# A hybrid decoder step on one core: the stretch from the third window attention to the memory attention laid out anew

## The reference

```python
for g, (w, d) in enumerate(B_GROUPS):          # ((128, 1), (512, 4), (2048, 16))
    if wins is None:
        o, lse = _dilated_prompt(qd[:, :, g], k_all[:, :, g], v_all[:, :, g], d, w // d)
    else:
        o, lse = _dilated_decode(qd[:, :, g], wins[g][0], wins[g][1],
                                 k_all[:, :, g], v_all[:, :, g], d, w // d)
    outs.append(o)
    lses.append(lse)
wts = jax.nn.softmax(jnp.stack(lses, axis=0), axis=0)
ydil = jnp.einsum('gbth,gbthd->bthd', wts, jnp.stack(outs, axis=0).astype(jnp.float32))
y_mix = ydil.reshape(B, T, B_WIDTH).astype(x.dtype) * jax.nn.silu(zg)
...
ym = _mem_attention(qm.reshape(B, T, M_HEADS, M_HDIM), mk, mv).reshape(B, T, M_WIDTH) * jax.nn.silu(zm)
out = jnp.concatenate([y_mix, ym], axis=-1) @ w_out
x = x + _rmsnorm(out, p['g_post'][l])
```

## Time and profile before

| | us |
|---|---|
| median of 3 runs | 1996.47 (1989.38 to 1996.92) |
| the profiled execution | 1994.59 |
| its span, first to last instruction | 1992.8 |
| PE busy (94%) | 1882.9 |
| DVE busy (40%) | 795.9 |
| ACT busy (25%) | 502.7 |
| POOL busy (22%) | 444.4 |

### The profile page before, as it was taken

How to read it: one execution, slowest core, us unless ns; L and a number is a source line. 1 busy time by engine, 2 the same in 40 slices (tenths; PEclk the granted TensorE clock), 3 DMA queues, 4 the chain that set the end, 5 groups by cost and what they waited for, 6 DMA issues and landing times.

```text
span 1992.8 us, 20946 instructions
## 1 busy us (share of the span) xinstructions
PE 1882.9 (94%) x8106; PEld 1381.9 (69%) x8117; DVE 795.9 (40%) x1463; ACT 502.7 (25%) x1122; POOL 444.4 (22%) x353
## 2 busy tenths in 40 slices
PE   7999999899999999979999999999999978699798
PEld 4566654687666667746658888888888866578373
DVE  0332202454455523552242552354345324855333
ACT  1412222554233323401210013211211222123211
POOL 0000000110222101230004663276237522122100
PEclk9999999999999999989999999999999988899899
DMA  7321210122756433641111111222233235524322
GB/s 260 106 69 59 69 39 13 55 77 39 225 162 193 153 106 89 171 143 64 44 52 43 43 53 50 80 96 75 64 101 111 88 94 157 173 89 141 121 85 86
DMA packets 163165, 196.13 MB, mean 98 GB/s; under 512 B 19355, under 2 KB 122395, under 8 KB 162930
## 3 DMA queue, kind: packets, MB, share of 16 engines
q1 hardware_dynamic: 135748, 168.83, 26.9%
q10 hardware_dynamic: 27318, 25.95, 4.3%
HBM read 156.97 MB, written 37.85 MB: 98 GB/s over the span
## 4 chain that ended last, share of the span: by engine, by line
PE 85%; DVE 6%; DMA 3%; ACT 3%; issue 2%; POOL 1%; ACTq 1%; SPq 0%; POOLq 0%; DVEq 0%
PE PS L2718 25%; PE PS L301 20%; PE PS L1908 10%; PE PS L502 4%; PE PS L1941 4%; PE PS L1768 3%; PE PS L381 3%; PE PS L1621 2%; PE PS L512 2%; DMA window_outputs<-WK 2%; PE PS L1656 1%; PE PS L1633 1%; PE PS L783 1%; PE PS L775 1%; PE PS L1653 1%
## 5 line engine op out<-in xcount | busy, mean ns | idle before, releaser
L301 PE MATMUL PS<-HT,RING 128*128 128x344 f32 x1344 | 391.2, 453 | 1.6 <-DVE HT L459 1.2
L301 PEld LDWEIGHTS PS<-HT,RING 128*128 128x128 f32 x1344 | 255.0, 190 | 135.7 <-DVE HT L459 2.0
L2718 PE MATMUL PS<-HT,RING 128*128 128x260 f32 (+1 forms) x1152 | 300.3, 389 | 11.0 <-ACT BIG L2802 11.0
L2718 PEld LDWEIGHTS PS<-HT,RING 128*128 128x128 f32 x1152 | 216.1, 195 | 41.0 <-ACT BIG L2802 12.7
L1908 PE MATMUL PS<-BIG 128*128 128x512 f32 x384 | 173.4, 603 | 0.0
L1674 ACT ACTIVATE WK<-PS,WK 128x256 f32<-128x256 f32 (+1 forms) x160 | 68.9, 436 | 237.4 <-DVE WK L1694 237.4
L1908 PEld LDWEIGHTS PS<-BIG 128*128 128x128 f32 x384 | 72.1, 193 | 81.3 <-issue 81.1
L2321 POOL TENSOR_TENSOR RING<-RING,VEC 128x1024 f32<-128x1024 f32 x48 | 92.3, 1947 | 135.6 <-DMA RING<-in_w_in_b 73.8
L2802 ACT ACTIVATE BIG<-PS 128x256 f32<-128x256 f32 (+1 forms) x96 | 37.0, 385 | 302.9 <-PE PS L2718 302.8
L728 POOL TENSOR_TENSOR WK<-WK,CST 128x512 f32<-128x512 f32 x8 | 10.3, 1287 | 422.0 <-DMA WK<-mlstm_rows 422.0
L1694 DVE TENSOR_REDUCE WK<-PS 128x2 f32<-128x512 f32 (+1 forms) x80 | 48.3, 603 | 135.4 <-PE PS L1621 90.6
(11 more groups left out here) (334 smaller groups left out, 2927.9 us busy)
## 6 DMA issues: line engine op xcount, KB each, us to landing
WK<-in_cache_mem_kv SPq DMA_DIRECT2D x64, 256.0 KB, 4.7
RING<-in_w_kv_b SPq DMA_DIRECT2D x12, 1024.0 KB, 5.4
RING<-in_w_in_b SPq DMA_DIRECT2D x12, 1024.0 KB, 5.2
WK<-in_cache_win SPq DMA_DIRECT2D x48, 256.0 KB, 4.8
RING<-in_w_in_a ACTq DMA_DIRECT2D x21, 512.0 KB, 4.2
RING<-in_w_mkv SPq DMA_DIRECT2D x16, 512.0 KB, 4.9
BIG<-in_x_prompt SPq DMA_DIRECT2D x16, 512.0 KB, 3.2
XTRA<-in_state_C SPq DMA_DIRECT2D x32, 256.0 KB, 3.7
```

Of the source, the lines that this page charges most:

```text
L301: last = nc.tensor.matmul(PS[:, s + b, 0:SEG], w[:, kt * P:(kt + 1) * P], rhs(kt, b * SEG, (b + 1) * SEG), start=(kt == 0), stop=(kt == kt ...
L2718: last = nc.tensor.matmul(PS[:, bank, 0:mid - lo], weight_block(u // 2, s, k), h_block(u % 2, t, k), start=(k == 0 and j not in (2, 3, 6)) ...
```

## The change

Stores of the window outputs go from SP to ACT. Row statistics get a buffer of their own, `ROWSTAT`, with four blocks, and are copied into `OUTR` only with the second half of the output, so the wait for the store moves from the maximum to the copy of the output. The eight keys of the third window are loaded by two transfers of four tiles into `LATE_KEYS`, and their queries get three buffers. Of each "D" value ACT multiplies two tiles in 8 instructions of 128x128 (one per head), and DVE multiplies one. "B" gets four key tiles, two query tiles and two product tiles; two of each and more of these lie where pieces 6 and 7 of `w_out_b` go, so these two are loaded by SP after the last key sum. The slots of nearly everything after 257 are set anew, the first two window attentions get a step every 2 slots, and the value places and the DVE order of layer A's output stage are moved.

```diff
+        def whole_group(name, n):
+            return name == "D" and n >= 2 * NS
+        def query_held(name, n):
+            if name == "D":
+                return max(2 * NS, n - 2) if whole_group(name, n) else n
+            return n - (len(SMP[name]["queries"]) - 1) * per_query(name)
...
+            if n == 2 * NS and name == "D":
+                sp.wait_ge(sig("rotated").sem, 24)
+                for half in range(2):
+                    at = slice(4 * half, 4 * half + 4)
+                    sp.dma_start(LATE_KEYS[:, at, :], wins[2][at, :, 0, :].rearrange("b p n -> p b n"))\
+                        .then_inc(key_loaded(name, n + 4 * half)[0], 16)
...
-            for t in range(nt):
+            for t in range(1 if name == "D" else nt):
...
+                if name == "D" and t == 1:
+                    dve.wait_ge(*scaled_by_act("value", b))
...
+        def sample_values_act(act, name, b):
+            c = SMP[name]
+            v = value_tiles(name, b)
+            act.wait_ge(*value_loaded(name, b))
+            for t in range(1, c["nt"]):
+                for h in range(H):
+                    x = v[t][:, h * P:(h + 1) * P]
+                    at = t * HP + h * NS + b
+                    last = nc.scalar.activation(x, x, ACT.Copy, scale=c["m"]["turned"][:, at:at + 1])
+            last.then_inc(sig("scaled_by_act").up(), 1)
...
-                if g not in MEM and s % 2 == 0 and (g > 0 or i >= 2):
-                    dve.wait_ge(*(out_stored(g, i - 2) if i >= 2 else out_stored(g - 1, 6 + i)))
...
+                    if pair == 0 and (g > 0 or i >= 2):
+                        dve.wait_ge(*(out_stored(g, i - 2) if i >= 2 else out_stored(g - 1, 6 + i)))
+                    if pair == 1:
+                        nc.vector.tensor_copy(OUTR[:, i % 2, 512:520], ROWSTAT[:, i % 4, :])
...
-        VALUE_SLOTS = {"A": {(1, 2): 0, (1, 4): 1, (1, 6): 2, (0, 9): 3, (0, 11): 4, (1, 9): 5, (1, 11): 6, (2, 1): 7},
+        VALUE_SLOTS = {"A": {(1, 2): 0, (1, 3): 1, (1, 5): 2, (1, 6): 3, (0, 8): 4, (0, 9): 5, (0, 11): 6, (1, 8): 7},
...
-            first, second = (5, 8) if x == "A" else (2, 5)
+            first, second = (8, 8) if x == "A" else (2, 5)
...
-            if a < 3:
-                return 84 * (a + 1) + 5 + 5 * s // 3
-            return 313 + 3 * s // 2
+            if a < 2:
+                return 84 * (a + 1) + 5 + 2 * s
+            return 257 + 3 * s // 2 if a == 2 else 315 + 4 * s // 3
...
-            return 84 * (g + 1) + 20 + 7 * j if g < 2 else 266 + 3 * j
+            return 84 * (g + 1) + 20 + 7 * j if g < 2 else 265 + 2 * j
...
-            return [b for b in range(NS) if 292 + 2 * b == x]
+            return [b for b in range(NS) if 286 + 3 * b == x]
...
-            return [c for c in range(8) if 291 + 2 * c == x]
-        SHARES, SCORES_D, PROBS_D, TURN_MKV, QUERY_B, B_KEYS = 287, 288, 291, 311, 312, 313
+            return [c for c in range(8) if 292 + 5 * c // 2 == x]
+        SHARES, SCORES_D, PROBS_D, TURN_MKV, QUERY_B, B_KEYS = 284, 283, 285, 314, 315, 316
...
-        def store_outputs(sp, g, i):
-            sp.wait_ge(*count("out_read", unit(g, 2 * i + 2)))
-            sp.dma_start(output_rows(g, i), OUTR[:, i % 2, :]).then_inc(sig(f"outputs{i % 2}_saved").sem, 16)
+        def store_outputs(act, g, i):
+            act.wait_ge(*count("out_read", unit(g, 2 * i + 2)))
+            act.dma_start(output_rows(g, i), OUTR[:, i % 2, :]).then_inc(sig(f"outputs{i % 2}_saved").sem, 16)
...
+            sp.wait_ge(sig("key_sums").sem, SMP["B"]["base"] + 2 * NS)
+            for n in range(6, KT):
+                load_piece(sp, n)
...
-            for c in merged_at(x - 4):
+            for c in merged_at(x - 3):
                 merged_turn_pe(pe, c)
...
+                for w, s in steps_at(x - 1):
+                    if w < 3 and s >= 3 and s % 2 == 1:
+                        store_outputs(act, w, (s - 3) // 2)
...
-                for c in merged_at(x):
+                for c in merged_at(x - 1):
                     merge_dve(dve, c)
-                for b in values_at(x):
+                for b in values_at(x - 1):
                     sample_values_dve(dve, "D", b)
...
-                if B_KEYS + 4 <= x < SLOTS and x % 3 == 1:
+                if B_KEYS + 4 <= x < SLOTS and x % 2 == 1:
```

More of the change, by code:

```diff
@@ L1215, in build @@
         tile_loaded = [sig(f"tile{n}_loaded") for n in range(4)]
-        query_loaded = [sig(f"query{n}_loaded") for n in range(2)]
+        query_loaded = [sig(f"query{n}_loaded") for n in range(3)]
         def samples(name, nt, base, key, value, query, tiles, queries, prods, misc, free, new=None, bank=None,
@@ L1264, in count_loads @@
                 for k in range(c["nt"] * NS):
-                    buf = k % len(c["tiles"])
-                    n[buf] += 16
+                    buf = key_buffer(name, k)
+                    if not whole_group(name, k) or k % 4 == 0:
+                        n[buf] += 16
                     LOADS[name, "key", k] = n[buf]
@@ L2433, in stat_of @@
                 return NMAX[:, 2 * s:2 * s + 2], TOTAL[:, 2 * s:2 * s + 2]
[L2434 removed]
+            return tuple(ROWSTAT[:, i % 4, at + 2 * pair:at + 2 * pair + 2] for at in (0, 4))
         def out_stored(g, i):
@@ L2519, in layer_b_sp @@
                     store_rows(sp, g, i)
-                for w, s in steps_at(x - 1):
-                    if w < 3 and s >= 3 and s % 2 == 1:
-                        store_outputs(sp, w, (s - 3) // 2)
-                for n in keys_at(x + 6):
-                    if n % NS == 0:
-                        sp.wait_ge(sig("query_rows_saved_d").sem, 16 * (n // NS + 1))
+                for n in keys_at(x + 5):
                     sample_load(sp, "D", n)
+                if x == SHARES - 1:
+                    sp.wait_ge(*count("out_ready", unit(2, 16)))
+                    for b in range(2):
+                        value_load(sp, "D", b)
                 if x == SHARES:
@@ L2534, in layer_b_sp @@
                         load_merge(sp, c)
-                    for b in range(2):
-                        value_load(sp, "D", b)
                     sp.wait_ge(sig("rotated").sem, 24)
@@ L2563, in layer_b_sp, with load_piece @@
             out_sp(sp, "B")
+        def load_piece(engine, n):
+            engine.dma_start(OUT["B"].piece(n), a["w_out_b"][0][n * P:(n + 1) * P, :])\
+                .then_inc(sig("out_weights_loaded").sem, 16)
         def rotated_before(u):
@@ L2803, in product_copy_act, with scaled_by_act @@
                                  ACT.Copy).then_inc(sig("projections_copied").up(), 1)
+        def scaled_by_act(kind, n):
+            order = [(what, k) for x in range(SLOTS) for what, at in (("merge", merged_at), ("value", values_at)) for k in at(x)]
+            return sig("scaled_by_act").sem, order.index((kind, n)) + 1
         def merged_act(act, c):
@@ L2853, in layer_b_act @@
                     act.wait_ge(sig("yd_ready").sem, 1)
-                if n >= 0 and n % 2 == 0 and n // 2 < KT:
-                    n //= 2
-                    act.dma_start(OUT["B"].piece(n), a["w_out_b"][0][n * P:(n + 1) * P, :])\
-                        .then_inc(sig("out_weights_loaded").sem, 16)
+                if n >= 0 and n % 2 == 0 and n // 2 < 6:
+                    load_piece(act, n // 2)
             complete(act, NUNIT - 1)
```

59 lines of the change are left out of this document (38 added, 21 removed).

## The result

The changed kernel takes 1923.95 us (median of 4 runs, 1922.78 to 1924.54) against 1995.39 for the kernel before beside it: ratio 0.9647, 95% interval 0.9626 to 0.9668. The profiled execution takes 1923.77 us with a span of 1921.7; before, it was 1994.59 and 1992.8. The forecast was 1920.

What follows compares the result with a forecast made beforehand. PE, 94% busy, was taken to lose time to waits and the half clock behind them. Gains 14.3 + 7.5 + 20.5 + 23.5 + 0 + 8.8 = 74.6 us from 1994.6 give 1920 us, range 1900 to 1944.

Steps and rivals of the forecast that it cites:

- Layer A's output stage: PE's 10.83 us wait for value 5 and the half clock behind it go; gain 14.3 us, bounds 0 and 14.3.
- First two attentions: First two window attentions: exp gets 1.74 us more, waits for late stores go; gain 7.5 us, bounds 3 to 8.7.
- Third attention: Third window attention: ACT's stores, keys without waits and later buffer reuse end the store waits; gain 20.5 us, bounds 8 to 22.
- Rival 3: Stores land late rather than issue late, third attention keeps its 20.5: 1940; or layer A's values come late: 1934; chance 0.09.
- Rival 4: ACT, in order at stores, value and merge loads, holds everything and its late copies stop PE: 2040 us; chance 0.03.
- From the softmax of "D" to the memory attention: DVE sheds value multiplies to ACT and only its bursts hold PE; gain 23.5 us, 16 of 39.5 left, bounds 5 to 36.
- Merge loads land in 4.3 us: Softmax of "D" to memory attention: merge loads have 2 slots, costing 0 to 1 us each on ACT, unseen by PE.
- The 8 us for POOL's pass over pair 22: Behind slot 293, POOL's pass over weight pair 22 slows a merge from 2.31 to 6.27 us; 8 us for wait and half clock.
- Rival 1: DVE stays the bound behind slot 283, 26 to 32 us lost there instead of 16: about 1933 us; chance 0.20.
- rival 2: Clean stretch behind slot 283: loss shrinks from 16 to 5 us, third attention's from 3.4 to 1.5: 1907; chance 0.10.
- Memory attention: Memory attention, 70.4 us: steps closer but same work, no gain taken; bounds -4 and 2 us.
- Layer B's output stage: Start of layer B's stage: "B" key sum wait and half clock go (13.1), waiting for `w_out_b` pieces costs 4.3; gain 8.8, bounds 3 to 13.

Runs made afterwards that it cites:

- the run of its two lines alone: The kernel before with only layer A's value places and DVE's order in its output stage as changed; 1980.88 us, ratio 0.9925.
- the run of the split wait: The changed kernel with the wait for pieces 6 and 7 of `w_out_b` moved to where they are used; 1915.23 us, ratio 0.9611.

## Why the prediction was right, and where its steps were not

The time came out as forecast, and six of the seven stretches of the table to within 1 us. Agreement that close is in part luck: the same stretches of the kernel before differ by up to 4 us between two executions, and the forecast was summed from the one execution with which the table compares. Of the mechanisms, that of layer A's stage was right as it stood, those of the third attention and of layer B's stage in part.

*Layer A's output stage.* Right, 14.2 for 14.3 (14.4 from the stage's first matmul on), and shown by the run of its two lines alone.

*First two attentions.* Right, 2.8 and 4.8. Which of the moved steps brings it was not taken apart further; the stores alone bring 1.0 and 3.1 of it (100.5 and 92.2 us between the same slots).

*Third attention.* The size was right, 21.0 for 20.5, but I named three things that take the turn of the earlier trace rows apart as if all three were needed. The stores on ACT alone give all of it, and the rest of the change gives it without them. The statistics apart and the later copy give nothing measurable beside the stores on ACT. Rival 3, that a store is late because it lands late and so the move does nothing, saw something true that I had passed over: the three stores that held DVE for 18.4 of its 25.4 us did land late, in 5.0 to 6.6 us. It falls all the same, because this too came from the place behind a load, and went with the move. I had read 2.6 us from copy to issue in the earlier trace rows and stopped there, where the landing had the larger part. As to the sentence of the Trainium skill that I weighed there (DMA: Bandwidth & Descriptors, Issuing engines are not separate DMA queues), that a second issuing engine only saves the time of starting transfers: the move gave 22 us here, not the 8 us of issue, as the stores no longer stood at another transfer's wait, nor landed behind it.

*Rival 4, ACT as the queue that holds everything.* ACT carries 24 stores and 64 scalings more and takes 39.06 us of 88.20; PE never waits for an ACT copy of a product there, and with the stores back on SP the time is the same.

*From the softmax of "D" to the memory attention.* I left 16 of 39.5 us. Between the slots 20.1 are gained, so 19.4 are left; but the stretch also holds less work, 118 woven matmul records for 141, and at the 0.11 us of one in the forecast that is 2.5 us which only moved to the stretches on either side (10 and 13 records more). So some 22 us are lost there now. Three steps failed, in part against each other:
- "Merge loads land in 4.3 us ... which PE doesn't see". They land in 5.9 at the median and 8.1 at the worst, behind value loads and a pair load in SP's order, and the last one's lateness is half of the longest wait. I had taken the landing time of the old order for a stretch in which more is loaded in less time (DMA share 0.53 for 0.48, 178 for 155 GB/s).
- The 8 us for POOL's pass over pair 22. The mechanism was right and the place wrong: the costly pass is that over pair 23, on the last merge, in slot 312, where the pass and the late load together cost 7 to 8 us. At pair 22 the waits are 2.5 and 0.8 us, and without the pass PE waits for merge 2 instead. I had walked the slots for passes over values and had not asked for each pass which merge lies in it.
- The probabilities of "D", for which my sum has no term. They cost 9.2 - 6.8 = 2.4 us, by a PE wait of 1.8, since POOL's pass over pair 21 begins in them and slows DVE (below); with the pass moved, 1.0 us of this came back behind them.

Of my smaller terms, 1 to 1.5 us for each slot with a value and a merge (293, 305, 308) came out near in the sum and unevenly in the parts: no wait of 0.4 us or more behind 293, 2.6 us behind 305 in slot 307, where the merge also began 1.3 us late for its load, and 0.6 behind 308. The 1 to 2 us for the window output did not show: PE has no wait of 0.4 us or more in slots 313 to 315.

Rival 1 (DVE the bound, 26 to 32 us left) and rival 2 (a clean stretch, 5 left) both fall: DVE is busy for 62.75 of 88.20 us, and PE's waits are seven, with 14.8 us in all.

*Memory attention.* Right, 66.3 in both.

*Layer B's output stage.* The sum was right, 8.2 for 8.8, but by two errors that offset each other. The wait is where the forecast put it, and its term was mis-sized: counted from the start of slot 335, where the forecast's 6.2 us for the stage's start is 6.6, the two pieces are issued at 5.8 us and not 8.8 - 4.5 = 4.3, and the second lands 6.5 us after its own issue (1782.5 to 1789.0), not 4.5. So PE waits 5.98 us and then takes 9.87 for 16 matmuls, 8.7 us in all by the run of the split wait, where I had 4.3. On the other side I had 13.1 us, the wait for the "B" keys and the half clock behind it, and left out a wait that the kernel before has ahead of it, in slot 335:

```profile
1845.82 1.12 PE L1633 MATMUL PS<-CST,WK 128*128 128x128 f32 x4 [2.43 <-DVE WK L1703]
```

With the half clock behind this one, the stage's first matmul comes 10.3 us after the start of slot 335 before, and 6.6 us where nothing holds it (the run of the split wait). These 3.7 us go too: 13.1 + 3.7 - 8.8 = 8.0, against 8.2 in the table.

## What to carry to other kernels

A transfer can be late by what stands ahead of it in its queue: look at what the issuing engine stood at when the data was ready and at which transfer was issued just before, then move the transfer, or take away what it stood behind. Look at the landing time of the transfers that were waited for, for a median over all hides them. When a cause is removed and the time stays, look in the new trace for the second cause that ends at nearly the same moment, and remove both before either is called harmless. And for each pass of POOL over SBUF ask which work of DVE with inputs in SBUF lies under it, for POOL could be held back by a few slots at its last pass, and the kernel gained. Ask at the same time what the pass will meet in its new place: held back at pair 21, it met a value, and part of the gain was lost.

## What the runs showed of the hardware

The same eight merge instructions on DVE (128x128, both tensors in SBUF) take 2.31 us alone, 5.51 when they begin 4.7 us into POOL's pass, and 9.76 when they begin together with its scaling. The first of the eight in that last case (the timelines of that run from 1694.3 to 1696), and POOL's instruction beside it:

```profile
1694.19 2.07 DVE L3011 SCALAR_TENSOR_TENSOR BIG<-BIG,SM 128x128 f32<-128x128 f32 x1
...
1694.22 1.90 POOL L2367 TENSOR_TENSOR RING<-RING,VEC 128x1024 f32<-128x1024 f32 x1 [28.95 <-DMA RING<-in_w_in_b]
```

An instruction that takes 0.34 us alone ends 0.15 us after the POOL instruction that it met. The next six each end 0.14 to 0.15 us after another instruction of POOL's in the same way, and take 1.98, 1.42, 1.34, 1.33, 1.15 and 0.54 us; the eighth, with POOL done, takes 0.34. The Trainium skill (SBUF — State Buffer, Who interferes with whom) speaks of an exclusive lock for a whole instruction; this trace agrees. What the runs add is the price: a short DVE instruction pays for the whole of the POOL instruction that it meets, here up to six times its own time, and eight in a row pay for a whole pass, four times theirs.

Small instructions of another kind suffer too. DVE's and POOL's timelines of the changed kernel at the probabilities of "D":

```profile
1623.52 2.50 DVE L1411 TENSOR_SCALAR XTRA<-CST,XTRA 32x32 f32<-32x32 f32 x3
...
1619.51 3.77 POOL L2367 TENSOR_TENSOR RING<-RING,VEC 128x1024 f32<-128x1024 f32 x2 [10.81 <-DMA RING<-in_w_in_b]
1623.35 1.27 POOL L2383 TENSOR_TENSOR WK<-RING 128x512 f32<-128x512 f32 x1
```

Three instructions of 32x32 take 2.50 us beside POOL's sums; with the pass moved behind them they take 0.52 us. One by one they take 1.13, 1.30 and 0.22 us, and the first two end 0.03 us after one of POOL's sums each: it is a wait for an instruction, not a slower rate.

A store of 128x520 behind a load pays for the load. Of the 24 stores of the kernel before, 18 land in 2.0 to 2.3 us. The other six, three behind a weight pair and three behind a query, were issued 0.4 us after a load on SP; they take 5.0 to 7.4 us, and each lands 0.7 to 0.8 us after the load ahead of it. With the stores alone on ACT, the three issued 0.02 us after SP's load of a pair take 4.3 to 4.5 us where SP's three took 5.7 to 7.4, so the other engine softens this and does not end it.
